# A mixer, routed experts and two attention layers in one kernel: the first block begins by channel halves, and steps move behind the work that waits for them

## The reference, cut to what matters

```python
proj = rmsnorm(x, norm_mix_g) @ w_in                   # 1024 -> 2560
a_in, a_b, a_c, b_val, b_gate = split(proj)            # 512 channels each
y_a = a_b * depthwise_conv(a_c * a_in, conv_a_w)       # 3 taps: the narrow one
u = depthwise_conv(b_val * sigmoid(b_gate), conv_b_w) + conv_b_bias   # 31 taps: the wide one
y_b = silu(layernorm(u, ln_b_g, ln_b_b))
y = concatenate([head_rmsnorm(y_a, 8, beta_a), head_rmsnorm(y_b, 8, beta_b)])
x = x + y @ w_out
# routing: the group by argmax, in it the two best of 8 experts; a token's place with an
# expert is the count of earlier tokens that chose it
out += combine[:, e] * (silu(t @ w1[e]) * (t @ w3[e]) @ w2[e])       # e = 0..31
# per layer of the second block
y = sigmoid(g0) * (o_a @ w_up_a) + sigmoid(g1) * (o_b @ w_up_b) + sigmoid(g2) * (o_c @ w_up_c)
x = x + y @ w_out
x = x + memory_cross_attention(rmsnorm(x), rmsnorm(mem, mem_norm), w_q_x, w_kv_x, w_o_x)
x = x + swiglu(rmsnorm(x), w_gu, w_down)
```

## Time and profile before

| | |
|---|---|
| median of 3 runs | 1706.75 us (1703.9 to 1710.45) |
| profiled execution, device time | 1708.82 us |
| its span | 1706.8 us |
| mean granted TensorE clock | 0.976 of full |
| TensorE busy | 1605.6 us (94%) |
| VectorE busy | 881.8 us (52%) |
| ScalarE busy | 613.1 us (36%) |
| HBM read | 386.34 MB, 227 GB/s over the span |

### The profile page before, as it was taken

One profiled execution on the slowest core, in us unless ns is written; L12 is line 12 of the kernel. 1 busy time (PEld: TensorE's weight loads), 2 busy tenths in 40 slices (PEclk: granted clock), 3 DMA queues, 4 the chain that ended last, 5 costly groups with the idle time before them and its releaser, 6 DMA issues.

```text
span 1706.8 us, 25188 instructions
## 1 busy us (share of the span) xinstructions
PE 1605.6 (94%) x10754; PEld 1284.9 (75%) x10754; DVE 881.8 (52%) x1280; ACT 613.1 (36%) x973; POOL 58.2 (3%) x28
## 2 busy tenths in 40 slices
PE   7997989888989999998899899999999899899998
PEld 6886434443434479887788799999988778799998
DVE  5953212121211287677545676647668755476653
ACT  2123212111211154544513544435463532454443
POOL 0000000000000000060000000000024000000000
PEclk9998999999999999999999999999999999999999
DMA  9065999999999985426222655474625314266551
GB/s 366 12 247 222 429 429 429 429 427 429 429 429 427 423 295 181 142 101 216 99 99 100 204 191 171 163 259 153 216 102 178 136 58 173 79 193 198 173 184 40
DMA packets 124544, 393.78 MB, mean 231 GB/s; under 512 B 4256, under 2 KB 55840, under 8 KB 111648
## 3 DMA queue, kind: packets, MB, share of 16 engines
q1 hardware_dynamic: 124448, 392.38, 60.7%
HBM read 386.34 MB, written 1.05 MB: 227 GB/s over the span
## 4 chain that ended last, share of the span: by engine, by line
PE 67%; DVE 15%; DMA 9%; ACT 6%; issue 4%; SPq 0%; DVEq 0%; ACTq 0%
PE psum L1204 11%; DMA ring<-w 7%; PE psum L950 7%; PE psum L953 7%; PE psum L951 7%; PE psum L1470 5%; PE psum L1269 4%; DVE outs L1894 3%; ACT wp L1556 2%; PE psum L1537 2%; PE psum L1540 2%; PE psum L1539 2%; PE psum L1167 2%; PE psum L911 2%; PE psum L981 2%
## 5 line engine op out<-in xcount | busy, mean ns | idle before, releaser
L950 PE MATMUL psum<-h_hi,w_hi 128*128 128x256 f32 x1456 | 362.9, 287 | 1.8 <-ACT outs L1559 1.4
L951 PE MATMUL psum<-h_hi,w_lo 128*128 128x256 f32 x1456 | 357.6, 283 | 0.0
L950 PEld LDWEIGHTS psum<-h_hi,w_hi 128*128 128x128 f32 x1456 | 279.6, 192 | 7.1 <-issue 4.9
L951 PEld LDWEIGHTS psum<-h_hi,w_lo 128*128 128x128 f32 x1456 | 279.7, 192 | 0.2
L617 DVE TENSOR_TENSOR w_lo<-raw_a,w_hi 128x1024 fp32r<-128x1024 f32 x170 | 204.9, 1223 | 132.8 <-ACT w_hi L1559 131.9
L1559 ACT ACTIVATE w_hi<-raw_a 128x1024 fp32r<-128x1024 f32 x186 | 193.2, 1053 | 192.9 <-PE psum L953 70.4
L953 PE MATMUL psum<-h_lo,w_hi 128*128 128x256 f32 x1456 | 204.2, 283 | 0.0
L1204 PE MATMUL psum<-ring,outs 128*64 128x512 f32 x720 | 167.8, 623 | 26.7 <-DMA ring<-w 25.4
L953 PEld LDWEIGHTS psum<-h_lo,w_hi 128*128 128x128 f32 x1456 | 187.8, 192 | 0.0
L1204 PEld LDWEIGHTS psum<-ring,outs 128*64 128x64 f32 x720 | 58.0, 144 | 133.8 <-issue 133.6
L2099 DVE SCALAR_TENSOR_TENSOR qk<-psum,rtok,qk 128x512 f32<-128x512 f32 x16 | 18.2, 1136 | 221.3 <-PE psum L1204 221.3
(11 more groups left out here) (290 smaller groups left out, 2499.4 us busy)
## 6 DMA issues: line engine op xcount, KB each, us to landing
ring<-w SPq DMA_DIRECT2D x76, 2048.0 KB, 16.1
raw_a<-w_in SPq DMA_DIRECT2D x20, 2048.0 KB, 8.0
...
```

Source lines behind the costliest of these rows:

```text
L950: mm(to, hi[:, k, :], h_hi[:, k, :], start=(k == 0), stop=False)
L951: mm(to, lo[:, k, :], h_hi[:, k, :], start=False, stop=False)
```

## The change

The first block's start: x is loaded and turned in two halves by channels, the first half-pieces of `w_in` come as loads of their own (`mix_part`), six transposes of the identity go ahead, and the products of the first 256 channels of piece 0 run over the first four channel chunks of x before the second half is scaled. The squares are taken from PSUM ahead of the copies to `xT`. The convolution: the narrow one, its product with piece 4 and the head norm's sums come before the last six wide taps. The memory: it stays as loaded in `outs`, is squared by ScalarE with a sum along the row, scaled there, and turned by TensorE between the last turned tokens and the ranks, with the gain applied on the copy out. The ranks' products take fp32r operands, and the addition to `rank` follows the number of passes. In the layers, two rope additions move from steps 10 and 11 to behind the scores of 13 and 14, and tanh from the gates' step to behind the exponential of that step (the last one to behind the sub-norm's root); the mixture of the first branch waits for its own gates only. Tenants of PSUM and the places of some tiles follow.

```diff
+            mix_part(0, slice(0, 4), slice(0, SEQ), win0_part[0])
+            mix_part(0, slice(4, KD), slice(0, SEQ), win0_part[1])
+            mix_part(1, slice(0, KD), slice(0, SEQ), win1_part[0])
+            sp.dma_start(consts[:, P:N_CONST], cst[:, P:N_CONST]).then_inc(consts_in, 16)
+            mix_part(0, slice(0, KD), slice(SEQ, HALF), win0_part[2])
+            mix_part(1, slice(0, KD), slice(SEQ, HALF), win1_part[1])
...
+                f(sq[:, half * 4:half * 4 + 4, :], view(duo(f"x{half}"), 0, 4, SEQ), ACT.Square).then_inc(x_squares, 1)
...
@@ -145,6 +148,7 @@
         steps += extra.get(s, [])
         if s < last:
             steps.append(("scores", s))
+        steps += behind.get(s, [])
         if first <= s - 1 < last:
             steps.append(("turn", s - 1))
         if first <= s - 2 < last:
@@ -173,9 +177,8 @@
...
         + without_last(attention(8, 24, {**gate_parts((9, 13, 17, 21), 12, 2),
-                                         10: [("gates", 12, 2, 1), ("rope", 3, "qc")],
-                                         11: [("gates", 12, 2, 2), ("rope", 4, "kc")],
-                                         20: [("gates", 14, 4, 3), ("square_b",)]}), ("apply", 23))
+                                         20: [("gates", 14, 4, 3), ("square_b",)]},
+                                  {13: [("rope", 3, "qc")], 14: [("rope", 4, "kc")]}), ("apply", 23))
...
-            pe.wait_ge(x_in, 16)
+            enter(pe, "win0")
+            for _ in range(6):
+                pe.transpose(duo("win0")[:, 0:P], ident, ident)
             transpose_tokens(("x0", "x1"), xtok)
-            pe.wait_ge(xg_half, 2)
             for half in range(2):
-                for i in range(2):
-                    if half == 0:
-                        arrived(pe, i)
-                        enter(pe, f"win{i}")
-                    block(i, f"win{i}", 2 * half)
-                    block(i, f"win{i}", 2 * half + 1).then_inc(half_done, 1)
-                    if half == 0 and i == 0:
-                        pe.wait_ge(consts_in, 16)
-                        pe.wait_ge(x_summed, 1)
-                        enter(pe, "n_mix")
-                        mm(duo("n_mix")[:, 0:SEQ], c("mean_model"), sums8[:], start=True, stop=True).then_inc(mix_sums, 1)
+                pe.wait_ge(xg_half, half + 1)
+                pe.wait_ge(win0_part[half], 16)
+                for o in range(2):
+                    last = block(0, "win0", o, range(half * 4, half * 4 + 4))
+            last.then_inc(half_done, 1)
+            pe.wait_ge(consts_in, 16)
+            pe.wait_ge(x_summed, 1)
+            enter(pe, "n_mix")
+            mm(duo("n_mix")[:, 0:SEQ], c("mean_model"), sums8[:], start=True, stop=True).then_inc(mix_sums, 1)
+            enter(pe, "win1")
+            for i, o, loaded in ((1, 0, win1_part[0]), (0, 2, win0_part[2]), (1, 2, win1_part[1])):
+                pe.wait_ge(loaded, 16)
+                block(i, f"win{i}", o)
+                block(i, f"win{i}", o + 1).then_inc(half_done, 1)
             whole(2)
             whole(3)
-            pe.wait_ge(mem_in, 16)
-            transpose_tokens(("mem0", "mem1"), mtok)
             whole(4)
-            pe.wait_ge(conv_ready, 1)
-            sums("ln_mean", c("mean_mixb"), cb, 4)
-            pe.wait_ge(mem_squares, 1)
-            sums("n_mem", c("mean_model"), mem_sq, KD)
-            pe.wait_ge(c_squares, 1)
-            sums("ln_var", c("mean_mixb"), sq, 4)
             pe.wait_ge(squares_a, 1)
             head_sums("hs0", 4)
...
+            pe.wait_ge(conv_ready, 1)
+            sums("ln_mean", c("mean_mixb"), cb, 4)
...
+                    if (i, o) == (0, 1):
+                        pe.wait_ge(c_squares, 1)
+                        sums("ln_var", c("mean_mixb"), sq, 4)
+                    if (i, o) == (1, 1):
                         pe.wait_ge(b_squares, 4)
                         head_sums("hs1", 0)
-                    if (i, o) == (1, 1):
+                    if (i, o) == (1, 2):
                         head_factors("heads1", 1)
...
+            enter(pe, "mem")
+            pe.wait_ge(mem_step, MEM_SCALED)
+            for j in range(4):
+                if j > 1:
+                    pe.wait_ge(mem_step, MEM_SCALED + j - 1)
+                to = view(duo("mem"), (j % 2) * 512, 2, SEQ)
+                for k in range(2):
+                    for t in range(TT):
+                        kk = 2 * j + k
+                        last = pe.transpose(to[:, k, t * P:(t + 1) * P], mtok[:, t, kk * P:(kk + 1) * P], ident)
+                last.then_inc(mem_turned, 1)
+
+            pe.wait_ge(order_ready, 1)
             pe.wait_ge(member_ready, 1)
             to = view(duo("wout0"), 256, 3, N_EXPERTS)
             mem_t = member.rearrange("p (t g) e -> p t (g e)", t=TT)
-            mm(to[:, 0, :], c("before"), mem_t[:, 0, :], start=True, stop=True)
-            for o, (a, b) in ((1, ("ones", "before")), (2, ("ones", "ones"))):
-                mm(to[:, o, :], c(a), mem_t[:, 0, :], start=True, stop=False)
-                last = mm(to[:, o, :], c(b), mem_t[:, 1, :], start=False, stop=True)
+            mm(to[:, 0, :], order[:, 0, :], mem_t[:, 0, :], start=True, stop=True)
+            for o, b in ((1, 0), (2, 1)):
+                mm(to[:, o, :], order[:, 1, :], mem_t[:, 0, :], start=True, stop=False)
+                last = mm(to[:, o, :], order[:, b, :], mem_t[:, 1, :], start=False, stop=True)
             last.then_inc(ranks_done, 1)
...
+            for j in range(4):
+                act_e.wait_ge(mem_turned, j + 1)
+                for k in range(2):
+                    kk = 2 * j + k
+                    last = f(memT[:, kk, :], view(duo("mem"), (j % 2) * 512, 2, SEQ)[:, k, :], ACT.Copy,
+                             scale=g1("mem_norm")[:, kk:kk + 1])
...
                         if w[3] == 3:
-                            g = w[2]
-                            act_e.wait_ge(gate_scaled, (l * 6 + g) * 2 + 2)
-                            part = gates[:, 4 * g:4 * g + 4, :]
-                            f(part, part, ACT.Tanh, scale=0.5).then_inc(gates_ready, 1)
+                            whole_gate = w[2]
...
+                        if whole_gate is not None:
+                            saturate(whole_gate, l)
+                            whole_gate = None
...
+                        saturate(whole_gate, l)
+                        whole_gate = None
...
-            convolve(cb, ub, range(TAPS_B - 6, TAPS_B), g1("conv_b"), g1("conv_bias"), (2, 3))
-            v.sem_inc(conv_ready, 1)
             convolve(yT[:, 0:4], ua, range(TAPS_A), g1("conv_a"), None, range(4))
-
-            v.wait_ge(mix_sums, 2)
-            v.tensor_tensor(cb, cb, spread(duo("ln_mean")[:, 0:SEQ], 4), ALU.subtract).then_inc(centred, 1)
-            v.wait_ge(centred, 1)
-            v.sem_inc(free_of("ln_mean"), 1)
             done_piece(v, 4)
             v.tensor_tensor(ab, view(duo("win4"), 0, 4, SEQ), spread(rstd[:], 4), ALU.mult).then_inc(free_of("win4"), 1)
             freed(v, "win4")
             v.tensor_tensor(yT[:, 0:4], yT[:, 0:4], ab, ALU.mult).then_inc(conv_a_ready, 1)
-
+            convolve(cb, ub, range(TAPS_B - 6, TAPS_B - 2), g1("conv_b"), g1("conv_bias"), (2, 3))
             v.wait_ge(mix_root, 2)
-            v.sem_inc(free_of("ln_var"), 1)
-            link(v.reciprocal(ln_r, std[:]))
-            v.wait_ge(mix_root, 3)
             v.sem_inc(free_of("hs0"), 1)
             v.reciprocal(roots[:, 0, :], roots[:, 0, :]).then_inc(factor_ready, 1)
-            for k in range(4):
-                v.scalar_tensor_tensor(cb[:, k, :], cb[:, k, :], g1("ln_g")[:, k:k + 1], ln_r, ALU.mult, ALU.mult
-                                       ).then_inc(yb_part, 1)
+            convolve(cb, ub, range(TAPS_B - 2, TAPS_B), g1("conv_b"), g1("conv_bias"), (2, 3))
+            v.sem_inc(conv_ready, 1)
...
+            v.wait_ge(mix_sums, 3)
+            v.tensor_tensor(cb, cb, spread(duo("ln_mean")[:, 0:SEQ], 4), ALU.subtract).then_inc(centred, 1)
+            v.wait_ge(centred, 1)
+            v.sem_inc(free_of("ln_mean"), 1)
+            v.wait_ge(mem_step, MEM_ROOT)
+            v.reciprocal(mem_factor, mem_std).then_inc(mem_inverse, 1)
+            v.wait_ge(mix_root, 3)
+            v.sem_inc(free_of("ln_var"), 1)
+            link(v.reciprocal(ln_r, std[:]))
+            for k in range(4):
+                v.scalar_tensor_tensor(cb[:, k, :], cb[:, k, :], g1("ln_g")[:, k:k + 1], ln_r, ALU.mult, ALU.mult
+                                       ).then_inc(yb_part, 1)
...
-            link(v.tensor_tensor(rank, rank, placed[:, 0:2, :], ALU.add))
             link(v.tensor_reduce(most, placed[:, 2, :], AX.X, ALU.max))
-            v.sem_inc(free_of("wout0"), 1)
...
-                        if b == 0:
-                            v.wait_ge(gates_ready, l * 6 + 6)
+                        v.wait_ge(gates_ready, l * 6 + 2 * b + 2)
```

115 lines of the change are left out of this document (65 added, 50 removed).

## The result

The changed kernel takes 1694.86 us (median of 6 runs, 1691.24 to 1697.35), the kernel before beside it 1706.76 (1703.9 to 1710.45): the ratio is 0.9929, with a 95% interval of 0.9915 to 0.9943. That is 11.9 us off, where 19.2 were forecast. The profiled execution has a span of 1693.8 us.

The account below looks back on a forecast made before the run. TensorE, busy 1605.6 of 1706.8 us, was taken as the bound. Terms of 5.2 + 2.0 + 1.2 + 11 = 19.4 us off the profiled 1708.8 gave 1689.4, and 2.05 less for the median 1687.5 us; range 1680 to 1698.

Parts of the forecast that it names:

- (a): Rival: the first block's gain stops at the experts, whose first weights are issued in the routing; 1696 us, 10%.
- the marks: Signs: first product near 9 us, gating near 25, second halves near 112, first gather near 142.5, SyncE's stream near 158.
- Change 1: First block's start: x in halves and first weights in parts bring the first products earlier; 5.2 us off, 3.6 to 6.8.
- The slow start: TensorE's first 16 products: 3.2 us lost to a slow start, of which half, 1.6 us, was taken as staying.
- Change 2: Memory's 16 transposes leave the convolution for TensorE's wait before the ranks: hidden with 1 us of room, else up to 2.
- Change 3: First block, narrow convolution first: the outputs' second halves begin 2.0 us earlier, with 0 to 3.3 as bounds.
- Change 4: Routing: rank products in fp32r give 0.95 us, the moved addition of the rank 0.25; 1.2 us in all.
- Change 5: Attention: rope additions behind the scores, tanh behind the exponential; 11 us off for both layers, bounds 4 and 13.
- (b): Rival: attention gives nothing, since the next wait, the exponential, takes over; 1698.4 us, 14%.
- (c): Rival: in attention the split behind tanh comes late and TensorE stands, 25 us lost instead of 11 gained; 1723 us, 4%.
- (d): Rival: arrivals in parts bring no earlier start since the queue works on all at once, and attention gives half; 1702, 6%.
- both of its own marks: Signs of a wrong prediction: experts' stream less than 5 us earlier, or waits for w_hi behind the tanh.

Follow-up runs that it names:

- e1: The kernel before with only the attention part of the change (rope additions and tanh moved): 1698.36 us, ratio 0.9948.
- e9: The changed kernel without its six transposes of the identity at the start: 1697.26 us, ratio 0.9945.
- e11: e8 with 11 identity transposes instead of 6 ahead of x and 4 more between its halves: 1668.42 us, ratio 0.9775.
- e12: e11 with VectorE's low half behind the scores in every attention step: 1666.13 us, ratio 0.9764.
- e10: The changed kernel with tanh back at the head of ScalarE's step, the rope additions left moved: 1699.02 us, ratio 0.9951.
- e2: The changed kernel with the attention order and tanh of before, so start, convolution, memory and ranks alone: 1702.29 us, ratio 0.9970.
- e4: The changed kernel with VectorE's low half behind the scores after a tanh, and ropes behind the scores of steps 10 and 11: 1680.33 us, ratio 0.9841.
- e5: The changed kernel with filler transposes of the identity where TensorE stands behind a moved tanh in attention: 1693.97 us, ratio 0.9923.
- e6: The changed kernel with only the rope additions moved, to behind the scores of steps 10 and 11: 1694.05 us, ratio 0.9926.
- e3: The changed kernel with filler transposes of the identity ahead of the first head sums, the ranks and the first gather: 1687.43 us, ratio 0.9882.
- e7: The changed kernel with the fillers of e3 and the two attention moves of e4 together: 1677.22 us, ratio 0.9822.
- e8: e7 with further fillers at head sums, head factors, gather, the layers' start and cross attention: 1668.90 us, ratio 0.9790.

## Why the prediction was right, and where it was not

The forecast was 1687.5 us with a range to 1698; 1694.86 lies in it, 7.4 us above its centre. Its mechanisms came true in the main and most of its sizes did not; the total alone, 1.1 us from rival (a)'s 1696, could not have told them apart. In the first block the marks fell short: second halves at 114.3 us (112 forecast), gather at 146.3 (142.5; the forecast's own terms give 151.97 - 8.4 = 143.6), stream at 162.0 (158).

**Change 1** was forecast at 5.2 us (3.6 to 6.8). The nine profiles with the new start (all but e1, e9, e11 and e12) have the gate 3.3 to 6.1 us ahead of the earlier trace rows; the middle one, 25.91, is 4.1 ahead, or 3.2 ahead of the 29.11 that the same start as before had in e1. The mechanism is right, and the size is within its bounds or just below. The slow start isn't a fixed price: the transposes of x's second half began at 7.5 to 8.65 us where 7.0 was forecast, and the products took 7.1 to 9.1 us. e11 and e12, with TensorE hardly standing, show 7.14 us, as the changed kernel's profile did. The Trainium skill, in "TensorE: Matmul & The Clock Gate", Part 1, says that the array's throttled state is the default and activity releases it. By that, all of the slow start could go, and the 7.14 us agree. The clock column can't confirm it: in the kernel before it shows 1.00 already from 13 to 17 us, where 6 records run in 2 us against 11 at the full rate. The first part of `w_in` was forecast to land at 8.4 us; only e11 waited for it, until 9.64.

**Change 2** was hidden as forecast, with 1.41 us to spare in this profile and 0.53 in others (e9, e10).

**Change 3** is the step that failed. "Head sums 1.95" and factors at the full clock rested on the earlier trace rows, taken where TensorE stood 0.74 us. In the new order TensorE stands 4.33 us ahead of them, and the text did not ask what its clock does there: without fillers the sums take 3.08 to 3.58 us and the factors 3.68. From the gate to the second halves the kernel before took 89.0 us, the changed one 90.4, and e2, e4, e5, e6, e9 and e10, with the same order, 90.0 to 91.4. With fillers e3 and e7, whose factors still ran at the lower clock, took 88.8 and 89.2, and e8, e11 and e12 87.3, 87.6 and 85.9. So the order held the 2.0 us, and the lower clock took them. The base was lucky as well: in e1 the old order took 92.0, with its clock fallen.

**Change 4**: from the first rank product to the choice of slots 3.75 us became 3.04, 0.7 where 1.2 was forecast. The same 3.04 stand in e3 at the full clock, so it isn't the clock: the addition to `rank` (144.46) moved behind the number of passes but still stands ahead of the choice (144.83), so its 0.25 us stayed, and VectorE stands 0.24 us behind its subtractions. The gather was taken at no change; its 1.3 us more, and the 2.6 us less in e3, are what "If the transposes keep the clock up" left open. The memory's transposes end at 140.4 and TensorE stands 1.41 and 3.45 us behind them.

**Change 5** was forecast at 11 us and measured 8.9 (e1), not clear of 11. The old waits went as forecast. The text saw that "behind tanh now stands the split of a chunk, 1.05 us later", and asked only whether TensorE would want that chunk. The one who wanted it was VectorE, for the low half, with the next scores behind it in its queue. The mark set for this, waits for w_hi behind tanh, was met there (0.96 us), though the text had looked for them at TensorE only. In e4, where that wait is gone, the kernel takes some 14 us less.

The rivals: (b), that attention gives nothing, is excluded by e1. (c) was half right in its cause, the late split, and wrong in its place and size. (a) does not hold: from the stream to the index products of layer 0 all fourteen profiles take 527.4 to 528.7 us, so what the stream gains, the layers begin earlier by. Of (d) neither cause came: the parts brought an earlier start and attention gave more than half, though the first block gave 5.1 of its 8.4. By both of its own marks the prediction was wrong: the stream's gain of 4.5 us is under its 5, and a wait for w_hi appeared behind the tanh. Its total came out in the range because that was wide enough for these shortfalls.
